# A later start for the three middle weight-sum jobs of a layer (two-layer encoder trunk, one Trainium2 core)

## What is computed

```python
for l in range(2):
    h = x @ w_in                            # q, k, v of both attentions, and two gates
    a = differential attention, 8 heads     # samples: 512 cached rows each, and their own
    b = sliding-window attention, 16 heads on 2 kv heads, window 128, with sinks
                                            # samples: cache_swa_k, cache_swa_v
    mix = (sigmoid(ga) * (a @ w_branch_a) + sigmoid(gb) * (b @ w_branch_b)) @ w_o
    x = layer_norm(ALPHA * x + mix)
    x = layer_norm(ALPHA * x + square(relu(x @ w_up)) @ w_down)
```

## Time and profile before

| | |
|---|---|
| median of the runs shown | 2153.51 us (2150.11 to 2153.92, 3 runs) |
| the profiled execution | 2153.98 us |
| its span, first to last instruction | 2152.2 us |
| mean granted TensorE clock | 0.994 |
| busy: PE, DVE, ACT, POOL | 99%, 68%, 57%, 3% |
| DMA, mean over the span | 186 GB/s |

### The profile page before, as it was taken

The page is one execution under the profiler, slowest core; times in us unless marked ns, Lnnn a source line. Parts: engine busy times, 40 slices in busy tenths (PEclk is TensorE's granted clock), DMA queues, the critical chain, the costliest instruction groups (busy, mean ns, idle before and its releaser), DMA issues.

```text
span 2152.2 us, 38215 instructions
## 1 busy us (share of the span) xinstructions
PE 2122.7 (99%) x15004; PEld 1940.8 (90%) x15004; DVE 1470.2 (68%) x2336; ACT 1229.0 (57%) x2493; POOL 65.2 (3%) x100
## 2 busy tenths in 40 slices
PE   9999999999999999999999999998899999999998
PEld 7998889999989898989889888898899898989897
DVE  6757778667879356665767677785668793566646
ACT  4457776587535356656234677674875353556561
POOL 1000000000000000000010000000000000000000
PEclk9999999999999999999999999999999999999999
DMA  8876567984351855454268775479842517554541
GB/s 262 246 271 251 209 240 208 269 261 109 94 186 45 237 155 173 146 170 138 103 215 235 286 253 200 182 230 258 242 119 84 186 57 230 158 171 153 171 148 69
DMA packets 100866, 399.27 MB, mean 186 GB/s; under 512 B 15272, under 2 KB 16936, under 8 KB 87600
## 3 DMA queue, kind: packets, MB, share of 16 engines
q1 hardware_dynamic: 67904, 191.55, 26.0%
q0 software_dynamic: 7936, 92.28, 17.2%
q10 hardware_dynamic: 24848, 112.99, 14.7%
HBM read 367.42 MB, written 118.23 MB: 226 GB/s over the span
## 4 chain that ended last, share of the span: by engine, by line
PE 93%; DMA 2%; ACT 2%; issue 1%; DVE 1%; ACTq 0%; DVEq 0%
PE PS L828 9%; PE PS L830 8%; PE PS L829 8%; PE PS L1049 7%; PE PS L1050 7%; PE PS L1051 7%; PE PS L917 5%; PE PS L918 5%; PE PS L919 5%; PE PS L987 3%; PE PS L988 3%; PE PS L989 3%; PE PS L861 3%; PE PS L863 3%; PE PS L862 3%; PE PS L1177 2%
## 5 line engine op out<-in xcount | busy, mean ns | idle before, releaser
L828 PE MATMUL PS<-xt_hi,w_hi 128*128 128x320 f32 x1184 | 384.2, 325 | 8.8 <-ACT rope_s L1628 8.6
L830 PE MATMUL PS<-xt_hi,w_lo 128*128 128x320 f32 x1184 | 367.6, 310 | 0.0
L829 PE MATMUL PS<-xt_lo,w_hi 128*128 128x320 f32 x1184 | 367.5, 310 | 0.0
L2541 DVE TENSOR_TENSOR w_lo<-w_raw,w_hi 128x1024 fp32r<-128x1024 f32 x146 | 176.7, 1221 | 149.0 <-ACT w_hi L1579 147.6
L2548 DVE TENSOR_TENSOR w_lo<-w_raw,w_hi 128x1024 fp32r<-128x1024 f32 (+1 forms) x176 | 199.2, 1138 | 114.9 <-ACT w_hi L1595 114.6
L1579 ACT ACTIVATE w_hi<-w_raw 128x1024 fp32r<-128x1024 f32 x146 | 152.8, 1059 | 175.5 <-PE PS L1051 155.6
L828 PEld LDWEIGHTS PS<-xt_hi,w_hi 128*128 128x128 f32 x1184 | 224.6, 190 | 14.3 <-ACT rope_s L1628 9.0
L829 PEld LDWEIGHTS PS<-xt_lo,w_hi 128*128 128x128 f32 x1184 | 224.9, 190 | 0.1
L830 PEld LDWEIGHTS PS<-xt_hi,w_lo 128*128 128x128 f32 x1184 | 224.1, 189 | 0.0
L1595 ACT ACTIVATE w_hi<-w_raw 128x1024 fp32r<-128x1024 f32 (+1 forms) x176 | 172.2, 985 | 86.1 <-PE PS L989 66.3
L1049 PE MATMUL PS<-w_hi,act_a_hi 128*128 128x512 f32 x480 | 187.6, 391 | 0.0
(11 more groups left out here) (391 smaller groups left out, 5096.7 us busy)
## 6 DMA issues: line engine op xcount, KB each, us to landing
w_raw<-in_weights SPq DMA_DIRECT2D x186, 512.0 KB, 5.0
kc<-in_k_cache ACTq DMA_DIRECT2D x32, 1024.0 KB, 7.8
vc<-in_v_cache ACTq DMA_DIRECT2D x16, 2048.0 KB, 8.7
w_raw<-up_sums SPq DMA_DIRECT2D x112, 256.0 KB, 2.9
up_sums<-in_up_blocks POOLq DMA_DIRECT2D x24, 1024.0 KB, 10.4
w_raw<-in_up_blocks SPq DMA_DIRECT2D x84, 256.0 KB, 2.8
down_sums<-in_down_blocks POOLq DMA_DIRECT2D x16, 1024.0 KB, 8.8
w_raw<-in_down_blocks SPq DMA_DIRECT2D x32, 512.0 KB, 3.5
```

Source lines behind the costliest of these rows:

```text
L828: mm(out, wh, hi[:, k, c], start=(k == 0), stop=False)
L829: mm(out, wh, lo[:, k, c], start=False, stop=False)
L830: last = mm(out, wl, hi[:, k, c], start=False, stop=(k == KT - 1))
L2541: v.tensor_tensor(w_lo[slot][:], raw[:, raw_of(s, n)[0], :], w_hi[slot][:].bitcast(F32), ALU.subtract)\
```

## The change

The job "down 1" of each layer no longer waits until the last head's cached values are consumed, but until both window caches of the layer have landed. Up 2 and down 2 follow it as before.

```diff
@@ -804,7 +804,7 @@
                 if (kind, part) == ("up", 0):
                     pool.wait_ge(w_ready[0], nth(l, AT_V) + 1)
                 elif (kind, part) == ("down", 1):
-                    pool.wait_ge(dec_pv, 2 * HEADS * (l + 1))
+                    pool.wait_ge(swa_cache_loaded, 32 * (l + 1))
                 elif (kind, part) == ("up", 3):
                     pool.wait_ge(w_ready[0], down_at(l, 0) + 1)
                 (up_sums_of if kind == "up" else down_sums_of)(l, part, JOB_TRANSFERS * j)
```

## The result

The changed kernel takes **2131.1 us** (median of 4 runs, 2128.01 to 2132.67) against 2153.72 us for the kernel before on the same chip (4 runs, 2150.11 to 2157.53): a ratio of 0.9891, 95% interval 0.9875 to 0.9906. It is faster by 1.1%. The forecast was 2127.2 us with a range from 2122 to 2142: the time lies inside, 3.9 us above the forecast. The profiled execution took 2132.67 us, its span is 2130.9 us, the mean granted clock 0.999 (before 0.994).

What follows compares the result with a forecast made beforehand. TensorE (PE), busy 2122.7 of 2152.2 us, bounds the kernel, so only its idle or slow-clock time can be won. From 2153.98 us, minus 13.6 (branch A) and 13.2 (window entry), gives 2127.2 us; range 2122 to 2142.

Steps and rivals of the forecast that it cites:

- (a): Branch A, both layers: gate fetches landing late beside the jobs cost PE idle time and clock; 13.6 us to be won.
- (b): Window-stage entry, both layers: value cache issue L2431 held behind key cache and job packets; costs 13.8 us, 13.2 to be won.
- jobs in their new place: Window stage and branch B: three jobs of some 50 us each, from 430 to about 580 us, cost 0.
- x: Window entry: time L2431 takes to issue on ACT, taken as 2.4 us after the change; 4.79 and 8.03 before.
- the formula: Window entry: PE's idle time per layer equals L2431's issue time minus 2.1 us.
- The slack of the gates: Branch A: without jobs, gate fetches land in 2.9 us against 3.9 us of slack, so ACT does not wait.
- The rule against the sum: Window entry: transfers below 512 B per piece miss line rate; if the 256 B pieces held L2431, 2140.4 us.
- rival 1: Window entry: the stall stays because the cache's own packets hold L2431; 2140.4 us, chance 0.12.
- the sign given for that: Branch A: in the changed kernel's profile, no ACT wait at L2250 over 1 us.
- Branch B: Branch B: gate fetches beside the moved jobs cost 0; the first has 7.9 us of slack, with 2.37 us ACT idle behind.
- one of the signs of a wrong forecast: Branch B: the forecast is wrong if ACT waits at L2250 there.
- Slower: Branch B: gate fetches land so late that ACT, then PE, stand still; 2157 us at 15 us a layer, chance 0.04.

Runs made afterwards that it cites:

- The early start: Against the changed kernel, the middle jobs start some 8 us earlier, at branch A's last gate, just ahead of the cache loads: 2146.75 us, 0.9946 of the kernel before.
- the split: Against the kernel before, down 1 starts where it did, while up 2 and down 2 wait for both window caches: 2132.47 us, ratio 0.9879.

## Why the prediction came out as it did

Time saved up to a given instruction, from the start of each in both traces, tells what each term was worth.

| term | forecast | measured |
|---|---|---|
| (a) branch A, layers 0 and 1 | 6.2 + 7.4 | 6.5 + 7.7 |
| (b) window entry, layers 0 and 1 | 5.5 + 7.7 | 5.7 + 8.0 |
| jobs in their new place | 0 | -2.0 - 0.8 |
| not the change's: start-up, a head's key cache | 0 | -2.0 - 2.0 |
| sum | 26.8 | 21.1; the spans differ by 21.3 |

For (a), in layer 0 the first sigmoid of branch A starts 1.76 us later than before and the keys' issue 4.73 us earlier, so 6.5 us were won between them. For (b), the issue of `rows` is 10.4 us earlier, 5.7 more. DVE's L3007, for which the second half of the output projection waits, starts only 8.46 us earlier: 2.0 lost. Layer 1 goes the same way (14.1, 22.1 and 21.3 us at the same places).

- **Where the time lay** was right: idle time and lost clock in two places per layer, and both terms came out within 0.6 us each. The early start showed (b) alone, the split (a) in part, and the kernel without jobs the sum of all.
- **The bounds of x.** I took 2.4 us between 0.34 and the 4.79 and 8.03 seen. It was 1.38 and 1.74: the 256-byte pieces took 73.5% of 2 us x 16 engines for 1316, 18 ns each, as before (19 ns); but ACT was free 2.1 us after the keys' issue, when they had not landed (4.8 us). It changed little: at x = 2.4 the formula leaves 0.3 us idle per layer, at 1.38 and 1.74 none.
- **The slack of the gates.** (a) went as forecast, but its reason holds only for most of the gates: the last one of branch A took 5.4 and 5.2 us against a slack of 3.9. ACT waited over 1 us for it in both layers, against the sign given for that, and PE did not.
- **The rule against the sum**, rival 1, is out. With no job beside it the load of small pieces held ACT for 1.4 us, and with two copies ahead for 8 us. That small pieces are slow for their bytes remains true here: 0.34 MB in 2 us is 168 GB/s, where the jobs' stretch had 275. It is not what stalls.
- **The step that was mis-sized: "The jobs in their new place. Each takes some 50 us ... from 430 to about 580 us ... 0."** The length came from the one job of the earlier trace rows that ran where little else did. The same rows had the three together: 335.65 to 500.59 us, 165 us and not 150; in the changed kernel they are issued from 431.84 to 596.22, 164 us. (Down 1 and up 2 took (543.44 - 431.84) / 2 = 55.8 us each, down 2 some 60 us.) So the jobs ended near 605 us and met the weight loads of the output projection, behind which DVE stands, and with it PE. The prediction looked for the cover in branch B and not in the stage behind. It cost 2.8 us in the profiled execution and 3.4 us between medians on one chip. PE's idle time fell by 14.8 us and not by 18 for this and for the key cache below.
- **Branch B** cost nothing, as forecast, but the cover was nearly used up, and not at the first gate, at which the prediction looked. That one landed in 4.4 and 5.4 us against its slack of 7.9; the second took 11.5 and 12.2 us where about 12 were free, and in layer 1 ACT waited 0.18 us for it, by the letter one of the signs of a wrong forecast. That nothing was lost there was closer than the 7.9 us suggested:

```profile
1630.34 0.74 ACT L2250 ACTIVATE rope_s<-rope_s 128x640 f32<-128x640 f32 x1 [0.18 <-DMA rope_s<-gates_kept]
```

- **The rest of the gap**, 4 us, are places that vary from run to run: the first head starts 1.96 us later than in the trace of before, and the two loads of the first key cache of layer 1 took 12.2 us to land (median) against 6.9. Up to these places the jobs start by the same conditions in both kernels, and two executions of one kernel (the one with down 2 moved) issue their first key cache at 117.0 and 115.7 us, as the others do at 115.4 to 117.4. A sum against one profiled execution carries such a spread, and the range had room for it.
- **Slower** never came near: PE waited for no gate of branch B.

## What to carry to other kernels

Background transfers cost where a late-issued load has little slack, not where the DMA share is high: here 0.80 for 94 us cost nothing, and 0.93 beside a 3.9 us slack cost 7 us a layer. When such work is moved, follow it to its new end with the length that the whole run of jobs has in the trace, and look there for the loads that are issued just in time (here the weights of the output projection). Here an issue behind a load of 2048 small pieces held ACT for 8 us when copies were queued ahead; starting the copies on the semaphore that says the load has landed cut that to 1.4 to 1.7 us. A late wait can hide behind a load that looks slower: `rows` took 19.2 us and nobody waited for it; the chain of waits names the load that counts.

## What the runs showed of the hardware

- A load of small pieces got nothing beside the first copy from DRAM to DRAM issued ahead of it: 0 packets in 6 us against two copies in pieces of 64 KB, 0 in 3 us against 120 pieces of 8 KB. Beside the second copy in 8 KB pieces it got one piece for one (61 against 63 in 1.5 us), which left it 5% of the engines' time. Cutting the copies moved the hold from 8.00 to 6.24 us; issuing them later moved it to 1.38.
- A piece of 8 KB takes an engine 0.36 us in a plain copy (120 pieces, 90.2% of 16 engines for 3 us); in the kernel before a piece of an adding transfer takes 0.67 us (256 of them and 32 small packets, 72.0% of 16 engines from 345 to 360 us, beside other loads).
- The hold stays with the place behind the many pieces: reordering two loads moved a 4.79 us hold from the values' issue to the next store's (3.33 us).
- Kernels with these stalls also vary more: 2145.78 to 2169.97 us over 12 runs for one, 2127.63 to 2128.95 over 4 for one without (the numbers of runs differ). The early start, whose stall is in one place per layer, lies between (6.3 us of spread over 6).
